# Forgetting attention in a hybrid encoder layer: decay of past keys taken from the block's first query, the exponential read straight from PSUM, another block order

## The reference

```
z = x @ w_in                      # q, k, v, f, gate, conv B/C/h/gate, mem q/gate
logf = log_sigmoid(f + b_f);  cum = cumsum(logf)          # per head, float32
s = q.k / sqrt(128) + cum[query] - cum[key],  causal      # 12 heads of 128
o_fox = softmax(s) @ v                                    # prompt: 2048 keys; sample: 1024 cached + 64 new keys
u = C * h;  y_conv = B * conv3(u)                         # 1536 channels, causal width 3
y = LN(alpha * x + (g1*Wf(o_fox*silu) + g2*Wc(y_conv*silu) + g3*Wm(o_mem*silu)) @ w_o)
```

## Time and profile before

| | |
|---|---|
| median of the three runs | 3448.47 us |
| the profiled execution, its own time | 3459.89 us |
| its span on the slowest core (core 4) | 3458.3 us |
| spans of the eight cores | 3434.4 to 3458.3 us |
| PE busy on core 4 | 3329.8 us, 96% |
| DVE, ACT, POOL busy | 1198.0, 915.5, 860.8 us |
| granted TensorE clock, mean | 0.984 to 0.990 |

### The profile page before, as it was taken

One profiled execution on the slowest core, in us unless ns is written; L12 is line 12 of the kernel. 1 busy time (PEld: TensorE's weight loads), 2 busy tenths in 40 slices (PEclk: granted clock), 3 DMA queues, 4 the chain that ended last, 5 costly groups with the idle time before them and its releaser, 6 DMA issues.

```text
span 3458.3 us, 54793 instructions; the slowest of 8 cores (3434.4 to 3458.3 us)
## 1 busy us (share of the span) xinstructions
PE 3329.8 (96%) x18998; PEld 1643.9 (48%) x18998; DVE 1198.0 (35%) x1989; ACT 915.5 (26%) x1571; POOL 860.8 (25%) x1045
## 2 busy tenths in 40 slices
PE   7899999999998999999999999999999999999997
PEld 4555555555544444444444444455544444444443
DVE  0476666667676222222211111111112232111465
ACT  1355555455554111111111111111113331111111
POOL 2233333333334222222200000222221113322233
PEclk9999999999999999999999999999999999999999
DMA  9634333433331313131224443866662115665643
GB/s 166 122 74 81 73 81 70 81 70 71 73 66 33 49 25 49 25 49 25 46 58 104 109 92 81 167 152 141 154 144 48 25 25 126 137 144 140 206 151 118
DMA packets 151702, 315.80 MB, mean 91 GB/s; under 512 B 32112, under 2 KB 57328, under 8 KB 146940
## 3 DMA queue, kind: packets, MB, share of 16 engines
q0 software_dynamic: 39232, 134.54, 24.5%
q1 hardware_dynamic: 112200, 177.76, 17.0%
HBM read 351.46 MB, written 95.32 MB: 129 GB/s over the span
## 4 chain that ended last, share of the span: by engine, by line
PE 88%; DMA 4%; issue 2%; DVE 2%; ACT 2%; POOL 1%; POOLq 0%; ACTq 0%; DVEq 0%; SPq 0%
PE bank L146 88%; DMA m_scr<-mt 1%; DMA xT<-xTp 1%; DMA fv_p<-v 1%; ACT ge L163 1%; DVE st L181 1%; DVE acc L173 1%; POOL aC L173 0%; ACT pt L163 0%; POOL pt L169 0%; DMA wcb<-wcM 0%; ACT k L168 0%; ACT rl L163 0%; POOL mt L173 0%; POOL pt L705 0%
## 5 line engine op out<-in xcount | busy, mean ns | idle before, releaser
L146 PE MATMUL bank<-xT,wcb 128*128 128x512 bf16 (+1 forms) x3840 | 728.2, 343 | 7.1 <-DMA wcb<-wcM 6.5
L146 PE MATMUL bank<-xT,cwb 128*128 128x512 bf16 (+1 forms) x3840 | 702.5, 343 | 8.9 <-DVE us L173 8.1
L146 PE MATMUL bank<-xT,wkqg 128*128 128x512 bf16 (+1 forms) x2880 | 608.3, 348 | 8.7 <-DMA wkqg<-wkqg 5.0
L146 PEld LDWEIGHTS bank<-xT,wcb 128*128 128x128 bf16 x3840 | 327.1, 98 | 370.3 <-issue 13.5
L146 PEld LDWEIGHTS bank<-xT,cwb 128*128 128x128 bf16 x3840 | 325.1, 98 | 373.4 <-issue 16.4
L173 DVE TENSOR_TENSOR mt<-bank,gt 128x512 f32<-128x512 f32 (+1 forms) x240 | 143.5, 598 | 1032.5 <-PE bank L146 883.5
L163 ACT ACTIVATE pt<-st,ncc 128x512 bf16<-128x512 f32 (+4 forms) x492 | 314.8, 647 | 427.0 <-DVE st L181 352.0
L163 ACT ACTIVATE gt<-bank,bm 128x512 f32<-128x512 f32 (+1 forms) x240 | 147.0, 612 | 969.0 <-PE bank L146 965.0
L146 PEld LDWEIGHTS bank<-xT,wkqg 128*128 128x128 bf16 x2880 | 245.4, 99 | 274.1 <-issue 35.2
L181 DVE SCALAR_TENSOR_TENSOR st<-bank,cq 128x512 f32<-128x512 f32 x480 | 291.3, 608 | 201.0 <-PE bank L146 172.9
L173 DVE TENSOR_TENSOR acc<-acc,pt 128x512 f32<-128x512 f32 (+3 forms) x396 | 260.7, 658 | 0.9 <-POOL pt L705 0.4
(11 more groups left out here) (137 smaller groups left out, 2543.8 us busy)
## 6 DMA issues: line engine op xcount, KB each, us to landing
m_scr<-mt SPq DMA_DIRECT2D x128, 256.0 KB, 2.2
pv<-m_scr SPq DMA_DIRECT2D x128, 256.0 KB, 5.5
cwb<-wc POOLq DMA_DIRECT2D x12, 2048.0 KB, 16.8
wkqg<-wkqg POOLq DMA_DIRECT2D x11, 1536.0 KB, 15.1
mw<-wm POOLq DMA_DIRECT2D x16, 1024.0 KB, 13.9
x<-xp SPq DMA_DIRECT2D x16, 1024.0 KB, 7.2
y_p<-rr SPq DMA_DIRECT2D x16, 1024.0 KB, 4.8
wcb<-wcC POOLq DMA_DIRECT2D x16, 896.0 KB, 10.8
```

The costliest lines, as they stand in the source:

```text
L146: return lambda e: e.matmul(out, lhsT=lhsT, rhs=rhs, start=start, stop=stop)
```

## The change

- **Past tiles.** The decay of a past key is taken relative to the first query of the block: the bias `nb` = first query's `cq` + `ncc`, one column for each tile, made by POOL (`make_bias`, three tiles after the previous head's block of the same number has ended). The ACT exponential reads the score bank directly with scale and bias; the DVE instruction and `st` fall away for these 24 tiles of a head. The remaining factor exp(cq - cq of the first query), the tile `fq`, is made by ACT (`make_decay`), multiplied into `acc` after the last past tile (DVE), and into the output at the block's end. For that past and diagonal tiles have output banks of their own, which DVE joins in two instructions.
- **Sample.** The cached keys' tile has eight ACT exponentials of 64 columns with a bias each in place of one DVE instruction and one exponential of 512; `csd` is gone. Its output and row sum take one projection bank and are joined by four small DVE instructions.
- **Order.** Blocks go 0, 1, 3, 2 (`POS` gives the buffers). The sample's tiles come right after block 0 (in head 0 after block 1), so the cache loads of the next head start there. Fill order follows: q and gate of block 2 last.
- **Block end.** hi is made by DVE, lo one tile later instead of two. LA is 4, there are nine `pt` and two `st` buffers.
- **Prologue.** A query projection of head 0 moves ahead of the transposes of the forget logits; the first cache load and `make_bias` of head 0 come ahead of the first tiles; `wv0`'s rows are padded.
- **Conv.** Each of the four small sample groups follows the four projections of one block, with buffers of its own.
- **End.** The last chunk's layer norm is done in four slices over DVE, ACT and POOL, each with its own output transfer.

```
-    NST, NPT = 3, 7
+    NST, NPT = 2, 9
...
+        dg = lambda tb: [(h, tb, kc) for kc in range(4 * tb, 4 * tb + 4)]
+        of = lambda tb: [(h, tb, kc) for kc in range(4 * tb)]
+        one, late = of(1) + dg(1), [(h, 4, 0), (h, 4, 1)]
+        tiles += dg(0) + (one + late if h == 0 else late + one) + of(3) + dg(3) + of(2) + dg(2)
...
+    def make_bias(h, tb):
...
+        S.add(POOL, TS(nb[p][:, c0:c0 + n], ncc[:, k0:k0 + n, h:h + 1].rearrange("p a b -> p (a b)"), ref, ALU.add),
+              reads=[rr, r_ncc], writes=[r_nb[p][tb]])
...
-            S.add(DVE, STT(stmp[st][:, n0:512], banks[sb_][:, n0:512], SCALE, cq[:, t0 + n0:t0 + 512], ALU.mult, ALU.add),
-                  reads=[bankr[sb_], r_cq[tb]], writes=[r_st[st]])
-            S.add(ACT, ACTF(pt[p][:, n0:512], stmp[st][:, n0:512], AF.Exp, bias=ncc[:, kc, h:h + 1]),
-                  reads=[r_st[st], r_ncc], writes=[r_pt[p]])
             if diag:
...
+            else:
+                c = NB0[tb] + kc
+                S.add(ACT, ACTF(pt[p][:], banks[sb_][:], AF.Exp, bias=nb[h % 2][:, c:c + 1], scale=SCALE),
+                      reads=[bankr[sb_], r_nb[h % 2][tb]], writes=[r_pt[p]])
...
+            for c in range(8):
+                S.add(ACT, ACTF(pt[p][:, c * NS:(c + 1) * NS], banks[sb_][:, c * NS:(c + 1) * NS], AF.Exp,
+                                bias=nb[h % 2][:, 24 + c:25 + c], scale=SCALE),
+                      reads=[bankr[sb_], r_nb[h % 2][4]], writes=[r_pt[p]])
...
+    def make_decay(h, tb):
+        src, rs, out, ro = (cq[:, tb * 512:(tb + 1) * 512], r_cq[tb], fq, r_fq) if tb < 4 else (cqs[h % 2][:], r_cqs[h % 2], fs, r_fs)
+        S.add(POOL, TS(nr[0][:, tb - 1:tb], src[:, 0:1], -1.0, ALU.mult), reads=[rs], writes=[r_nr[0][tb]])
+        S.add(ACT, ACTF(out[:], src, AF.Exp, bias=nr[0][:, tb - 1:tb]), reads=[rs, r_nr[0][tb]], writes=[ro])
...
+            if kc == 4 * tb - 2:
+                make_decay(h, tb)
+            if kc == 4 * tb - 1:
+                S.add(DVE, TT(A[:], A[:], fq[:], ALU.mult), reads=[rA, r_fq], writes=[rA])
             if last:
-                S.add(POOL, COPY(pt[hi][:], A[:]), reads=[rA], writes=[r_pt[hi]])
+                S.add(DVE, COPY(pt[hi][:], A[:]), reads=[rA], writes=[r_pt[hi]])
...
+                    S.add(DVE, TT(fq[:], banks[Of][:], fq[:], ALU.mult), reads=[bankr[Of], r_fq], writes=[r_fq])
+                    S.add(DVE, TT(fq[:], banks[Ob][:], fq[:], ALU.add), reads=[bankr[Ob], r_fq], writes=[r_fq])
...
-                later.append((i + 2, s1))
+                later.append((i + 1, s1))
...
-    LA = 3
+    LA = 4
...
-        for tb, (t0, tn) in enumerate(TBLK):
+        for tb in (4, 0, 1, 2, 3):
...
+            if tb == 4:
+                late = gs
+            else:
+                out += gs[0] + gs[1] + gs[2] + gs[3] + late[tb]
...
-        past_block = [f0 + 5, f0 + 3 + 6, f0 + 11 + 6, f0 + 25 + 6]
+        past_block = [f0 + 5, f0 + 3 + 6, f0 + 29 + 6, f0 + 13 + 6]
...
+            center(0)
+            S.add(DVE, lambda e: e.reciprocal(out=rstd[s][0:tn, :], in_=rstd[s][0:tn, :]),
+                  reads=[r_rstd[s]], writes=[r_rstd[s]])
+            scale(POOL, 0)
+            center(1)
+            scale(POOL, 1)
+            center(2)
+            scale(DVE, 2)
+            center(3)
+            scale(DVE, 3)
```

More of the change, by code:

```diff
@@ L463, in build @@
     pj = [0]
+    held = set()
     def nextbank():
-        b = (0, 1, 7)[pj[0] % 3]
-        pj[0] += 1
-        return b
+        while True:
+            b = (0, 1, 7)[pj[0] % 3]
+            pj[0] += 1
+            if b not in held:
+                return b
     def group(mm, ncols, evict, n=16, step=4, need=-1):
@@ L758, in finish_block, with row_recip, run_later @@
             ss, rs = sgs[h % 2][:], r_sgs[h % 2]
-        S.add(POOL, TT(ao[a][:, 0:qn], rl_, ss, ALU.mult), reads=[r_rl, rs], writes=[r_ao[a]])
+        S.add(POOL, TT(ao[a][:, 0:qn], rl_, ss, ALU.mult), reads=[rr, rs], writes=[r_ao[a]])
         t0 = tb * 512
         S.add(SP, DMA(a_scr[h, :, t0:t0 + qn], ao[a][:, 0:qn]), reads=[r_ao[a]], writes=[r_as[h][tb]], dmasem=d_ao[a])
[L763 to L768, removed]
+    rown, fown = [None], [None]
+    def row_recip(rl_, rr, src, rs):
+        S.add(ACT, ACTF(rl_, src, AF.Ln), reads=[rs], writes=[rr])
+        S.add(ACT, ACTF(rl_, rl_, AF.Exp, scale=-1.0), reads=[rr], writes=[rr])
+    def run_later(i):
         for due, fn in [x for x in later if x[0] <= i]:
@@ L771, in issue_PV, with next_decays @@
         later[:] = [x for x in later if x[0] > i]
+    def next_decays(i, h, tb):
+        if h + 1 < H:
+            load_cq(h + 1, tb)
+            later.append((i + 3, lambda: make_bias(h + 1, tb)))
+    def issue_PV(i):
+        h, tb, kc = tiles[i]
+        run_later(i)
         p = slots[i]
         assert pown[p] == i
-        if kc == 0:
-            obank[(h, tb)] = 4 + take("o", 3)
-        Ob = obank[(h, tb)]
         if tb < 4:
-            A, rA = acc[tb % 2], r_acc[tb % 2]
-            n0 = (kc - 4 * tb) * 128 if kc >= 4 * tb else 0
+            if kc == 0:
+                abuf[(h, tb)] = take("acc", 2)
+            part = 0 if kc < 4 * tb else 1
+            if kc == 0 or kc == 4 * tb:
+                obank[(h, tb, part)] = 4 + take("o", 3)
+            Ob = obank[(h, tb, part)]
+            A, rA = acc[abuf[(h, tb)]], r_acc[abuf[(h, tb)]]
+            n0 = (kc - 4 * tb) * 128 if part else 0
+            last = kc == 4 * tb + 3
             vv, rv = vslice(h, kc, 128)
-            S.add(PE, MM(banks[Ob][:, n0:512], vv, pt[p][:, n0:512], first, last), reads=[r_pt[p], rv], writes=[bankr[Ob]])
+            S.add(PE, MM(banks[Ob][:, n0:512], vv, pt[p][:, n0:512], kc == 0 or kc == 4 * tb, last or kc == 4 * tb - 1),
+                  reads=[r_pt[p], rv], writes=[bankr[Ob]])
             if kc == 0 and tb == 0:
@@ L828, in colsof @@
     def colsof(i):
-        h, tb, kc, first, last = tiles[i]
+        h, tb, kc = tiles[i]
         if tb == 4:
@@ L839, in main_pieces @@
         if h == 0:
+            load_cache(0)
+            for tb in range(1, 5):
+                make_bias(0, tb)
             for i in range(LA):
@@ L878, in conv_buffers @@
         conv["sx"] = b("sx", [128, 512], F32, [r_sx])
+        for n, rr in (("cgs", r_cgs), ("bgs", r_bgs), ("scs", r_scs), ("tbs", r_tbs)):
+            conv[n] = b(n, [128, NS], F32, [rr])
         up = conv["up"]
@@ L946, in conv_pieces @@
-            out += group(cmm(1, tb), tn, ev_c)
-            out += group(cmm(2, tb), tn, ev_h)
-            out += group(cmm(0, tb), tn, ev_b)
-            out += group(cmm(3, tb), tn, ev_g)
+                    S.add(ACT, ACTF(sc[:, 0:tn], sc[:, 0:tn], AF.Ln, bias=1.0), reads=[rsc], writes=[rsc])
+                    S.add(ACT, ACTF(sc[:, 0:tn], sc[:, 0:tn], AF.Exp, scale=-1.0), reads=[rsc], writes=[rsc])
+                    S.add(POOL, TT(sc[:, 0:tn], sc[:, 0:tn], sx[:, 0:tn], ALU.mult), reads=[rsc, r_sx], writes=[rsc])
@@ L971, in build @@
                     fill += g_group(n, 0, past_block[0])
[L972 to L975 removed]
+                    fill += q_group(n, 1, past_block[1]) + g_group(n, 1, past_block[1])
+            fill += q_group(n, 4) + g_group(n, 4)
+            for tb in (3, 2):
+                fill += q_group(n, tb, past_block[tb]) + g_group(n, tb, past_block[tb])
         else:
```

252 lines of the change are left out of this document (147 added, 105 removed).

## The result

The changed kernel takes 3506.44 us where the kernel before took 3448.47 beside it (medians of three executions each): 1.0173 times as long (95% interval 1.0148 to 1.0198), 58 to 60 us slower, against 47 us faster in the forecast. In several of the sets of runs, some executions or some of their cores were disturbed, with a granted clock down to 0.81 in stretches where the other cores had 0.95 to 1.00, and every time, ratio and median over cores leaves those out.

The account below looks back on a forecast made before the run. PE, 96% busy, was taken as the bound, so only its idle time and clock loss could fall. Attention -32, conv -8, transition -3.5, prologue -2.5, end -5, new costs +4: -47 us, 3448.5 to 3401 us, range 3372 to 3436.

Parts of the forecast that it names:

- third rival: Attention: POOL's `make_bias` waits for the `cqs` load and blocks v's casts; 4.3 us a head loses the gain; chance 0.04.
- Start of a head (-9): First tiles of each head: score stalls of 1.6 us instead of 2.4, -9 us over 11 heads (-21 to +12).
- Waits for hi and lo (-14): Attention: row sums' and value matmuls' waits for `pt`, 14.9 us, fall to 1: -14 us.
- Clock (-9): Attention: shorter stalls give back half of the granted clock's loss, -9 us (0 to -19).
- New costs (+4): Attention: banks freed by ACT, and cache loads beside weight loads where v's output transfers hold DVE: +4 us (0 to 15).
- Engine loads: Attention, per head: DVE net -7 to -8 us of some 56, ACT +4 us, from 42 to 46.
- Small parts (-19 in all): Outside attention: conv -8, row sum after the last tile -3.5, prologue -2.5, last normalisation -5 us.
- conv: Conv: interleaving large and small groups removes the matmuls' wait for the bank that DVE's `us` frees, -8 us.
- the transition: After the last attention tile: the row sum waits 1.4 us for DVE instead of 4.90 for POOL's cast, -3.5 us.
- the end: Last layer norm in slices: the last transfer leaves at about 3448.1 instead of 3453.16, -5 us.
- the start: Prologue: a query projection covers the transposes' wait for the forget logits, so the first value matmul comes 2.5 us earlier.
- The rival on a denser PE: Attention: a denser PE draws a lower clock, 13/16, adding 209 us, about 3610 us; chance 0.01.

Follow-up runs that it names:

- both_one: both, with the sample's tiles after block 1 in every head and the past output joined early: 0.9902 of the kernel before, attention 946.5 us.
- both: The changed kernel with `nr` on DVE and the sample's `make_bias` 14 tiles after its tile instead of 3: 1.0005 of the kernel before, attention 979 us.
- small2: The kernel before with only the early query projection, interleaved conv groups and sliced last layer norm: 0.9954 of the kernel before, attention 967 us.
- one_only: The changed kernel with only the sample's tiles after block 1 in every head and the early join: attention 973 us, no ratio.

## Why the prediction was wrong

**The step that failed is the third rival's "against".** I had the chain's first half, priced it at a whole gain lost, and gave it 0.04, because "5 to 8 us pass between the load's issue and `make_bias`, as long as its landing of 6.2". That landing was read where the load stood in the kernel before. The change moves it beside 2 MB of weight and cache loads, where it takes 14.7 us against the 6.2 of the earlier trace rows, and POOL waited 70.6 us on core 1. The other half of the argument held: POOL came to `make_bias` 7.5 us after the load's issue in head 5. I also followed the queue behind POOL only to the casts of v. The instruction behind `make_bias` that mattered was `nr`, which releases ACT and so every exponential. Measured, the chain is 1030 - 979 = 51 us of the stage, 4.7 a head. That the rival's 4.3 us a head lies near is luck: it was the forecast gain divided by eleven heads, not a sum of waits.

**Start of a head (-9): wrong in sign.** Score stalls ahead of tile 8 were 4.2 us a head on core 1 (mean of heads 1 to 11; 1.8 before, counted the same way) against the 1.6 for 2.4 of the forecast. The term that failed is the eight short exponentials at 0.28 us, set below the 0.314 of the nearest row: they take 3.14 us together, 0.40 from start to start, though each is 0.312 in the profile, and they stand just where PE has no fill. The Trainium skill ("ScalarE: Activation LUTs", What ACT_TABLE_LOAD costs) would have them at 0.24 each, an estimate from its figures of 1.9 us in all; the trace disagrees, as in it the short ones do not overlap. For one exponential of 512 columns with a pointer bias the same rule gives 0.71 us, an estimate, and the trace has 0.682. Having the sample's tiles there is worth 979 - 946.5 = 32.5 us of the stage. One exponential in place of the eight gave 18 of it; what the other 14.5 are was not told apart.

**Waits for hi and lo (-14): right**, 14.9 us on core 1 became 1.3. **Clock (-9): wrong in sign**, as it follows the stalls: on core 1, 0.02 x 956.5 = 19 us lost before, 0.04 x 1035.4 = 41 after, 0.01 x 949.7 = 9 in both_one. Where the stalls went, the gain forecast for the clock came.

**New costs (+4): too small.** The forecast knew that v's output transfers hold DVE and that the loads move beside them. In both, where POOL's chain is cut, PE waits 13.0 us for DVE's v on core 1, a wait that core 1 did not have in the kernel before.

**Engine loads.** ACT: +37 us in twelve heads on core 1 for +48 forecast, the exponential from PSUM 682 ns for 680. DVE: -48 us for about -90. About a third of the difference is in one group; the same additions took 780 ns on core 1 before:
```profile
L173 DVE TENSOR_TENSOR acc<-acc,pt 128x512 f32<-128x512 f32 x248 | 209.3, 844 | 8.3 <-DVE acc L173 0.5
```
Neither engine's load decided anything.

**Small parts (-19 in all): about right.** In the changed kernel, medians over cores: the stages behind attention -7.6 us for -11.5 forecast (conv as said; the transition missed, because after the last tile PE waits for other work of POOL and DVE than the cast), the end -3.1 for -5, the start -2 for -2.5. small2 has -16 in all.

**The sum.** Medians over cores of the attention stage: POOL's chain +51, the sample's place +32.5, together 83.5; the stage is +63, so the remainder is -20.5, where I had -28 for it with new costs. The split depends on the order of the cuts, as the two faults lengthen each other: taken the other way, by one_only, the place is 57 and the chain 26, with the same total. With the small parts' -13 that makes +50, and the two profiled executions differ by 3506.44 - 3459.89 = 46.6. The timed medians differ by 58.0, because the profiled one of before was 11.4 above its median. The design without the two faults ends at both_one's -34 us: inside the range I gave, short of 47.

**The rival on a denser PE** is not borne out: core 1's dense stages stay at a granted clock of 1.00, before and after.

## What to carry to other kernels

When an edit moves a load, its time to landing has to be read from loads that now stand beside it, not from its old row; it was 14.7 us against 6.2 here. Then follow each instruction that waits for it through its engine's queue to the first instruction that another engine needs, however small: 0.23 us of work behind one wait stopped three engines. Work that is done for the next head belongs in a place, or on an engine, where nothing of this head stands behind it, and short instructions in a row belong where the bound engine has fill.

## What the runs showed of the hardware

A DVE addition with both inputs in SBUF waits until POOL's `ao<-rl,sg` is over, if that has begun. On core 1 of the changed kernel the 149 additions `acc<-acc,pt` (128x512) that begin beside no POOL instruction take 0.68 us; the 25 that begin while POOL makes `ao<-rl,sg` take 1.57 in the mean, which is the 1.02 that POOL had left and 0.55. In the end of the span shown above, on core 4, two DVE instructions take 1.50 and 1.74 us beside POOL's additions and 0.74 when they are over. On core 1 in order of time:
```profile
556.15 0.68 DVE L173 TENSOR_TENSOR acc<-acc,pt 128x512 f32<-128x512 f32 x1
556.44 1.52 POOL L173 TENSOR_TENSOR ao<-rl,sg 128x512 bf16<-128x512 f32 x1 [1.03 <-DVE rl L173]
557.08 1.43 DVE L173 TENSOR_TENSOR acc<-acc,pt 128x512 f32<-128x512 f32 x1
```
The Trainium skill ("SBUF — State Buffer", Who interferes with whom) says that a DVE instruction with two inputs in SBUF contends with a GpSimd instruction that reads SBUF, and that the later one blocks; these rows agree (1.43 us against 0.68 just before, and POOL's instruction ends at 557.96, 0.55 us before DVE's).

A load of 32 KB took 4.8 to 6.2 us to land when it stood beside cache loads of 0.5 MB alone, 6.0 behind block 1, and 12.5 to 14.7 issued some 7 us behind a weight load of 1.5 MB, though that is in another queue. What holds it (that load, or its own queue) stays open.
